# Recurrent block of a four-layer fp32 network: the order of its column, gate and projection work

## The reference, cut to what matters

```python
def recurrent_block(h, norm_g, w_in, conv_w, conv_b, gate_w, gate_b, lam, w_out):
    u = rmsnorm(h, norm_g)
    z = u @ w_in                                   # 1024 -> 2048 columns
    y = jax.nn.gelu(z[..., :LRU_WIDTH])            # first 1024 columns
    xr = causal_conv(z[..., LRU_WIDTH:], conv_w, conv_b)   # last 1024, 4 taps
    hr = rg_lru(xr, gate_w, gate_b, lam)
    return (y * hr) @ w_out
```

## Time and profile before

| what | value |
|---|---|
| median of 3 runs | 1990.87 us (1989.08 to 1991.81) |
| the profiled execution's own time | 1990.26 us |
| span of that execution in the trace | 1988.5 us |
| mean granted TensorE clock | 0.966 |
| TensorE busy share of the span | 94% |
| recurrent block in the trace, first column product to the end of the first quarters | about 1283 to 1373 us |

### The profile page before, as it was taken

The page is one execution under the profiler, slowest core; times in us unless marked ns, Lnnn a source line. Parts: engine busy times, 40 slices in busy tenths (PEclk is TensorE's granted clock), DMA queues, the critical chain, the costliest instruction groups (busy, mean ns, idle before and its releaser), DMA issues.

```text
span 1988.5 us, 32234 instructions
## 1 busy us (share of the span) xinstructions
PE 1868.5 (94%) x13950; PEld 1665.7 (84%) x13950; DVE 1315.3 (66%) x1380; ACT 1010.2 (51%) x1195; POOL 263.0 (13%) x152
## 2 busy tenths in 40 slices
PE   7998999999999999699999999787999897889999
PEld 7988888999898898688888888684989795669998
DVE  5988765544598776488888998655544465945443
ACT  5672345433567234467667776545433345655331
POOL 0021002433002100000000000000525000004342
PEclk9999999999999999799999999898999998789999
DMA  6422345554333235288888988343554343015552
GB/s 262 145 107 86 128 177 204 180 192 162 116 136 107 97 127 190 97 304 323 322 324 326 346 335 322 143 175 141 181 197 149 117 170 127 1 64 212 180 191 74
DMA packets 50977, 359.89 MB, mean 181 GB/s; under 512 B 5776, under 2 KB 5904, under 8 KB 8464
## 3 DMA queue, kind: packets, MB, share of 16 engines
q1 hardware_dynamic: 50832, 357.79, 48.8%
HBM read 356.72 MB, written 1.05 MB: 180 GB/s over the span
## 4 chain that ended last, share of the span: by engine, by line
PE 56%; DVE 6%; ACT 2%; issue 1%; DMA 0%; DVEq 0%; ACTq 0%
PE banks L1281 56%; DVE ring_lo L2124 1%; DVE work L2783 1%; DVE work L2864 1%; DVE small L2868 1%; ACT work L765 1%; PE banks L1837 0%; DVE h_lo L2174 0%; ACT high L765 0%; ACT h_hi L765 0%; ACT scr L765 0%; PE banks L2017 0%; DVE more_lo L2124 0%; DVE work L2476 0%; ACT L765 0%
## 5 line engine op out<-in xcount | busy, mean ns | idle before, releaser
L1281 PE MATMUL banks<-h_hi,ring_lo 128*128 128x256 f32 x1664 | 471.2, 283 | 0.0
L1281 PE MATMUL banks<-h_hi,high 128*128 128x256 f32 x1520 | 439.0, 289 | 4.1 <-DVE h_lo L2174 3.3
L1281 PE MATMUL banks<-h_lo,high 128*128 128x256 f32 x1520 | 430.6, 283 | 0.0
L2124 DVE TENSOR_TENSOR ring_lo<-ring,high 128x2048 fp32r<-128x2048 f32 x154 | 352.7, 2300 | 90.8 <-ACT high L765 89.3
L734 POOL CAST g_hi<-hidden 128x256 fp32r<-128x256 f32 x66 | 151.9, 2302 | 1371.9 <-DVE hidden L2142 1371.9
L765 ACT ACTIVATE high<-ring 128x2048 fp32r<-128x2048 f32 x154 | 292.2, 1902 | 67.7 <-DMA ring<-weights_in 60.9
L1281 PEld LDWEIGHTS banks<-h_hi,ring_lo 128*128 128x128 f32 x1664 | 319.0, 192 | 0.0
L1281 PEld LDWEIGHTS banks<-h_hi,high 128*128 128x128 f32 x1520 | 291.9, 192 | 9.5 <-issue 5.3
L1281 PEld LDWEIGHTS banks<-h_lo,high 128*128 128x128 f32 x1520 | 292.0, 192 | 2.6 <-issue 2.4
L765 ACT ACTIVATE work<-banks 128x512 f32<-128x512 f32 (+5 forms) x133 | 85.6, 649 | 287.3 <-PE banks L1281 276.6
L2124 DVE TENSOR_TENSOR more_lo<-more,more_high 128x2048 fp32r<-128x2048 f32 (+1 forms) x86 | 189.6, 2218 | 38.0 <-ACT more_high L765 38.0
(11 more groups left out here) (273 smaller groups left out, 3739.9 us busy)
## 6 DMA issues: line engine op xcount, KB each, us to landing
ring<-weights_in SPq DMA_DIRECT2D x225, 1024.0 KB, 4.9
more<-weights_in SPq DMA_DIRECT2D x104, 1024.0 KB, 4.9
more<-weights_in SPq DMA_DIRECT2D x8, 512.0 KB, 4.3
ring<-weights_in SPq DMA_DIRECT2D x6, 512.0 KB, 4.9
consts<-consts_in SPq DMA_DIRECT2D x1, 2033.0 KB, 17.3
params<-params_in SPq DMA_DIRECT2D x1, 1162.5 KB, 10.9
x<-x_in SPq DMA_DIRECT2D x2, 512.0 KB, 3.8
out<-x SPq DMA_DIRECT2D x4, 256.0 KB, 2.0
```

The costliest lines, as they stand in the source:

```text
L1281: return pe.matmul(out_, lhsT, rhs, start=start, stop=stop, **kw)
L2124: tt(lo_of(g), ring_of(g), hi_of(g).bitcast(F32), SUB).then_inc(unit_lo, 1)
```

## The change

The stage list becomes: six units of columns (the four recurrent ones, then two gelu ones), the raw gate unit, the two last gelu units, then the projection's four. The helper `recurrent(n)` gives the n-th column unit in the new order. TensorE computes columns 0 to 4, gates 0 to 3, column 5, gates 4 to 7, columns 6 and 7. The gelu columns (4 to 7) go to banks 0 to 3, those of the projection, and each first-half quarter of the projection waits for the eviction from its bank. ScalarE evicts gelu columns 5 and 6 between "exps" and "root" of each half, and column 7 at the very end. VectorE's `low` operations stand between the convolutions.

```diff
-            ("lru_in", 8, False), ("lru_gate", 1, True), ("out2", NPROJ, True), ...
+            ("lru_in", 6, False), ("lru_gate", 1, True), ("lru_last", 2, False), ("out2", NPROJ, True), ...
+    def recurrent(self, n):
+        return self.at("lru_in", n) if n < 6 else self.at("lru_last", n - 6)
 ScalarE
-                for q in range(8):
-                    act.wait_ge(unit_used, first + q + 1)
-                    src = banks[:, 4 + q % 4, :]
-                    if q < 4:
-                        ins = f(w(Y_AT + 512 * q, 512), src, ACT.Gelu_apprx_tanh)
+                def evict(n):
+                    act.wait_ge(unit_used, units.recurrent(n) + 1)
+                    if n < 4:
+                        dst = w(Z_IN, KT, T + 4)[:, 2 * n:2 * n + 2, 3:3 + T]
+                        ins = f(dst, grid(banks[:, 4 + n, :], 2), ACT.Copy)
                     else:
-                        dst = w(Z_IN, KT, T + 4)[:, 2 * (q - 4):2 * (q - 4) + 2, 3:3 + T]
-                        ins = f(dst, grid(src, 2), ACT.Copy)
-                    chain.to(ins, ain_out, q + 1)
-                    if q < 5:
-                        split(first + q + 3)
+                        ins = f(w(Y_AT + 512 * (n - 4), 512), banks[:, n - 4, :], ACT.Gelu_apprx_tanh)
+                    chain.to(ins, ain_out, n + 1)
+                    if n < 5:
+                        split(units.recurrent(n + 3))
+                for n in range(5):
+                    evict(n)
                 act.wait_ge(LR_V.sem, LR_V.at("rate"))
                 for i in range(2):
...
                     run(ins, LR_A, f"exps{i}")
+                    evict(5 + i)
                     lru_root(i)
+                evict(7)
 TensorE, project_halves
-                for c in range(2):
-                    for a in range(TT):
+                for a in range(TT):
+                    for c in range(2):
+                        pe.wait_ge(ain_out, 5 + 2 * a + c)
                         sub(a, c, 0)
 TensorE, lru
+                def columns_of(n):
+                    out_ = banks[:, 4 + n if n < 4 else n - 4, :]
+                    two_tiles(units.recurrent(n), out_, norm=None if n else 4).then_inc(unit_used, 1)
+                def gates_of(heads):
+                    for h in heads:
+                        pe.wait_ge(lru_conv, h // 2 + 1)
+                        if h < 4:
+                            pe.wait_ge(ain_out, h + 1)
+                        else:
+                            pe.wait_ge(ag_out, h - 3)
...
+                for n in range(5):
+                    columns_of(n)
+                raw_ready(g_)
+                gates_of(range(4))
+                columns_of(5)
+                gates_of(range(4, 8))
+                columns_of(6)
+                columns_of(7)
 VectorE
-                for q in range(3, 8):
-                    low(lru0 + q)
                 run(dve.memset(z[:, :, 0:3], 0.0))
                 for q in range(4):
-                    dve.wait_ge(ain_out, 5 + q)
+                    low(units.recurrent(q + 3))
+                    dve.wait_ge(ain_out, q + 1)
...
+                low(units.recurrent(7))
                 for i in range(2):
...
+                    dve.wait_ge(ain_out, 6 + 2 * i)
                     run(tt(xr, r2, y, MUL), LR_V, f"done{i}")
```

More of the change, by code:

```diff
@@ L83, in stages @@
     return [*mixers(0), ("dense", 2 * PART_UNITS, False), *mixers(1), ("moe", NE * PART_UNITS, False),
-            ("lru_in", 8, False), ("lru_gate", 1, True), ("out2", NPROJ, True), ("f0", 2 * PART_UNITS, False),
+            ("lru_in", 6, False), ("lru_gate", 1, True), ("lru_last", 2, False), ("out2", NPROJ, True), ("f0", 2 * PART_UNITS, False),
             ("kv", 6, False), ("query_a", 2, False), ("cmp", 4, True), ("query_b", 2, False),
@@ L344, in ffn @@
             expert(w[:, :2 * FE][:, s], w[:, 2 * FE:][:, s], a["f_w_out_2"][l][s])
-    narrow(a["a_w_in_2"][0])
+    recurrent = np.concatenate([a["a_w_in_2"][0][:, D:], a["a_w_in_2"][0][:, :D]], 1)
+    narrow(recurrent[:, :6 * 2 * P])
     add(a["a_gate_w_2"][0].transpose(2, 1, 0, 3))
+    narrow(recurrent[:, 6 * 2 * P:])
     output(a["a_w_out_2"][0], True)
@@ L1112, in lru @@
                 run(f(small[:, 16:24], small[:, 16:24], ACT.Exp, scale=-1.0), LR_A, "lambda")
-                first = units.at("lru_in")
-                for q in range(8):
-                    act.wait_ge(unit_used, first + q + 1)
-                    src = banks[:, 4 + q % 4, :]
-                    if q < 4:
-                        ins = f(w(Y_AT + 512 * q, 512), src, ACT.Gelu_apprx_tanh)
-                    else:
-                        dst = w(Z_IN, KT, T + 4)[:, 2 * (q - 4):2 * (q - 4) + 2, 3:3 + T]
-                        ins = f(dst, grid(src, 2), ACT.Copy)
-                    chain.to(ins, ain_out, q + 1)
-                    if q < 5:
-                        split(first + q + 3)
+                def evict(n):
[3 more added lines that the diff above has]
+                        ins = f(dst, grid(banks[:, 4 + n, :], 2), ACT.Copy)
+                    else:
+                        ins = f(w(Y_AT + 512 * (n - 4), 512), banks[:, n - 4, :], ACT.Gelu_apprx_tanh)
[4 more added lines that the diff above has]
+                    evict(n)
                 act.wait_ge(LR_V.sem, LR_V.at("rate"))
@@ L1881, in lru @@
             def lru():
[L1882 to L1885, removed]
                 g_ = units.at("lru_gate")
-                raw_ready(g_)
[L1888 to L1897, removed]
+                def columns_of(n):
[8 more added lines that the diff above has]
+                            pe.wait_ge(ag_out, h - 3)
+                        for g in range(2):
+                            ins = mm(banks[:, 4 + h % 4, g * T:g * T + T], raw_rows(g_, 2 * KT)[:, 2 * h + g, :],
+                                     w(XR_AT + h * T, T))
+                        ins.then_inc(unit_used if h == KT - 1 else ag_full, 1)
+                for n in range(5):
+                    columns_of(n)
+                raw_ready(g_)
+                gates_of(range(4))
[3 more added lines that the diff above has]
+                columns_of(7)
                 project_halves(2)
@@ L2740, in lru @@
                 xr = w(XR_AT, KT, T)
-                lru0 = units.at("lru_in")
-                for q in range(3, 8):
-                    low(lru0 + q)
                 run(dve.memset(z[:, :, 0:3], 0.0))
                 for q in range(4):
-                    dve.wait_ge(ain_out, 5 + q)
+                    low(units.recurrent(q + 3))
+                    dve.wait_ge(ain_out, q + 1)
                     for i in range(TAPS2):
```

## The result

The changed kernel takes 1980.3 us (median of five, 1977.38 to 1981.93), the kernel before in the same session 1989.3 us (five runs, 1988.2 to 1991.81): a ratio of 0.9949, interval 0.9938 to 0.996. A second session beside the experiments gave 1977.75 against 1989.48 us, ratio 0.9946 (0.9933 to 0.9959). Forecast were 1978.8 us and 12.1 us gained; measured were 9.0 us in the first session and 11.7 in the second. The profiled execution of the changed kernel took 1980.3 us with a span of 1978.5, against 1988.5 before. The eleven executions of the changed kernel in the two sessions fall into two groups: six with a mean granted TensorE clock of 0.971 or 0.972 took 1975.8 to 1978.2 us, five with 0.967 to 0.970 took 1980.3 to 1981.9, and the median of the first session lies in the second group, that of the second session in the first.

What follows compares the result with a forecast made beforehand. TensorE, busy 94% of the span, bounds the kernel where it stops. Gains of 11.6 (start) + 2.8 (clock) - 1.0 (gelu 7 wait) = 13.4, less 1.3 for a table load, give 12.1: 1990.87 to 1978.8 us, range 1975.8 to 1983.2.

Steps and rivals of the forecast that it cites:

- The idle of 13.5 us: TensorE between the last gate and the projection, during the recurrence of heads 0 to 3; gelu columns were to fill it.
- done0: End of the half 0 recurrence on VectorE, which lets the projection start; forecast at 1338.0, 11.6 us earlier than before.
- the two landing waits: ScalarE waiting for column loads issued one unit later: about 4.2 us before split 6, 1.9 before split 7.
- The bill behind it: Next norm's first Sqrt needs a table load after gelu 7, 1.28 us on the chain, cutting 13.4 gained to 12.1.
- R1: Rival: a table switch between busy ScalarE neighbours costs twice the load time; 8.2 us gained, 1982.7 us; chance 6%.
- the wait of the fourth quarter: In the projection, the fourth quarter waits for gelu 7 to free its bank, a loss of 1.0 us.
- The 2.8 us are saved: Six projection quarters on the path would take 20.2 us at full clock instead of 23.04, saving 2.8.
- So I take full clock: TensorE's idle before the projection, 1.6 us, was taken as too short to bring the half clock.
- The start of the block: Columns 0 to 4 were taken to keep their profiled ends, the first at 1288.93.
- R2: Rival: loads land late, so ScalarE's splits wait longer; 6 us gained, 1984.9 us; chance 4%.
- R3: Rival: stage shortens but nothing behind it does, or an overlooked wait (f0's loads, sigmoids) undoes it; 1990.9 us; chance 3%.
- R4: Rival: TensorE's denser stretch from 1312 to 1360 is granted the half clock; slower, about 2019 us; chance 2%.

Runs made afterwards that it cites:

- order_only: Changed kernel with the new column order and banks but no interleaving, all eight column units ahead of all gates: 1992.58 us, ratio 1.001 to the kernel before.
- gates_later: Changed kernel with the gate unit eighth instead of seventh in the load list and gates 4 to 7 behind column 6: 1979.38 us, ratio 0.9939.
- late_split: Changed kernel with the last unit's split behind the first exps, its low behind the first square, gelu 5 behind the first root: 1975.54 us, ratio 0.9927.
- changed_again: The changed kernel run and profiled a second time with no edit: 1977.75 us, ratio 0.9946 to the kernel before.
- gelu_pair: Changed kernel with gelu 6 and 7 evicted together ahead of the second root: 1977.39 us, ratio 0.9939 to the kernel before.
- gap_filled: Changed kernel with two products that nothing reads added on TensorE behind column 7: one run of 1976.48 us, no comparison.

## Why the prediction was right, and what was off

The mechanism stands. The idle of 13.5 us was taken by column work (order_only puts it back), done0 came 49.2 us after column 0 where 49.1 were worked out, and the two landing waits on ScalarE had 4.16 and 1.93 us where 4.2 and 1.9 were forecast. That of these only the wait in front of split 7 matters is shown by gates_later and late_split.

"The bill behind it" was right to the digit: 1.27 us between changed_again and gelu_pair, forecast 1.3. So R1 is out, a switch between busy neighbours costs its 1.28. The Trainium skill, "ScalarE: Activation LUTs", "Table sets: the hidden batching unit", says to do all calls of one table set before those of the next; the trace agrees for the switch behind the block, with these 1.27 us. The 1.38 us of drain that the same page of the Trainium skill adds to a switch in "What ACT_TABLE_LOAD costs" do not show here: split 6 ends at 1314.45, the load starts at 1314.47 and gelu 4 at 1315.76. (Between gelu 5 and the next load stand 0.76 us, and the row puts them down to VectorE.) The switches in front of gelu 5 and gelu 6 are hidden behind VectorE's squares, as forecast, and the one in front of gelu 7 is part of the wait of the fourth quarter, forecast as 1.0 us.

Three terms were mis-sized:

- "The 2.8 us are saved": not all of the 2.8 was clock. I took 3.37 us for a quarter, the distance of two adds, and three or six times that for a run of quarters from its first product to the end of its last. That leaves out a fixed part. At full clock three quarters took 10.57 us in the trace where I had 10.1, whether TensorE had stood still for 2.01 us before them (changed_again) or for 0.28 (gap_filled), and 10.46 directly behind other products (late_split): 0.4 us belong to any such run, and only 0.1 to the start from idle. The six quarters with the wait took 21.9 where I had 21.2, the last three alone 10.6. That is the 0.7 us which the sixth quarter is late in the second profile. By the same count the half clock had cost some 2.3 us before, not 2.8 (23.04 less 20.2 and about 0.5, an estimate).
- "So I take full clock": an idle of 2.0 us was enough for the half clock in two of four profiles. Its cost at the sixth quarter was 0.7 us, because the wait for gelu 7 lay beneath it.
- The start of the block: 1.57 us later in the profiled run, from the half clock in the norm ahead of it and in the first products of column 0. This is outside the change, and moves in all kernels of the study.

10.7 (first profile) and 11.4 us (second) arrive at f0, against 12.1. The first is 12.1 - 0.7 - 0.7, the second 12.1 - 0.7. The spans differ by 10.0 (1988.5 - 1978.5): 10.7 less the later start of 1.57 is 9.1 us at the first split of f0 (1374.40 to 1365.29), and the remaining 0.9 arises behind it. It says nothing of the change: from that split to the end the kernel took 614.1 us before, 613.2 in the first profile and 611.0 in the second, and 611.0 to 615.4 over the nine profiles, with the same program there in all. R2 and R3 are out: each landing was as forecast, and f0's first split waited for no load. R4 is out: in the changed kernel and its interleaved variants 0.50 was never granted for more than 3.4 us between column 1 and the end of the projection. The two sessions gained 9.0 and 11.7 us by their medians, a difference larger than any of these terms, so the runs alone say only that 9 to 12 us were gained. The profiles confirm the terms of the forecast; its exact size is not shown.

## What to carry to other kernels

To fill a stall, look for work with a late deadline that sits ahead of it, and start the long chain as soon as its own inputs exist; to reorder the inputs without starting the chain between them gained nothing. When a unit is moved in a list of loads that share a few places, work out the new issue time of every load behind it: here critical work of ScalarE queued some four microseconds behind a landing, and moving one split was worth 2.6 us. Look also at which table set the block leaves loaded, since the next stage's first Sqrt paid for the last Gelu.

## What the runs showed of the hardware that was not expected

After an idle of 2.0 to 2.15 us TensorE was granted 0.50 (1.2 GHz) in two profiles of four for 3.4 us, and 1.00 in the other two; one and the same program (the changed kernel) showed it once each way. Where it came, the clock fell only after the projection had been running again for 0.8 us (changed kernel) or 0.7 (gelu_pair). In identical work ahead of the block the sixteen records of the norm's second turn took 2.05 us in six of nine profiles and 3.38 to 3.78 in three. Three quarters of the projection took 10.57 us at 1.00 after an idle of 2.01 us and of 0.28, and 10.46 directly behind other products, so a start from idle cost 0.1 us.
